# A hybrid decoder step on one core: an earlier count in the recurrent stage, and a first weight tile loaded by quarters

## The reference, cut to what matters

```python
def rmsnorm(x, g):
    y = xf * lax.rsqrt(jnp.mean(xf * xf, axis=-1, keepdims=True) + RMS_EPS)
    return (y * g).astype(x.dtype)
...
xn = rmsnorm(x, lp['g_mix'])
u = xn @ lp['w_in']
u_rw, u_ml, u_pool, u_gate = jnp.split(u, IN_SPLITS, axis=-1)
...
kk = k * k_k                                  # RWKV-7, per head of 64
kk = kk / jnp.maximum(jnp.sqrt(jnp.sum(kk * kk, axis=-1, keepdims=True)), 1e-12)
```

## Time and profile before

| | |
|---|---|
| median of 3 runs | 2074.45 us (2072.27 to 2074.98) |
| profiled execution | 2075.46 us, of which the span from first to last instruction 2073.7 us |
| mean granted TensorE clock | 0.956 |
| busy | PE 89%, weight loads 75%, DVE 46%, ACT 29%, POOL 19% of the span |
| front stage | 0 to about 479 us |
| recurrent stage | about 480 to 1160 us |

### The profile page before, as it was taken

How to read it: one execution, slowest core, us unless ns; L and a number is a source line. 1 busy time by engine, 2 the same in 40 slices (tenths; PEclk the granted TensorE clock), 3 DMA queues, 4 the chain that set the end, 5 groups by cost and what they waited for, 6 DMA issues and landing times. The chain is left out here.

```text
span 2073.7 us, 33699 instructions
## 1 busy us (share of the span) xinstructions
PE 1853.3 (89%) x13379; PEld 1549.4 (75%) x13379; DVE 944.5 (46%) x1521; ACT 596.7 (29%) x838; POOL 393.3 (19%) x362
## 2 busy tenths in 40 slices
PE   6999999998999999999999899999988877777775
PEld 6999999997777777877778799999977544443332
DVE  5553444546464563755646454545534122112113
ACT  3343223323133232332322433333434111000112
POOL 6550003112220212203212000084013000000002
PEclk9999999999999999999999999999998989888888
DMA  6445354434132222221221344543683999999995
GB/s 252 164 158 179 119 168 165 135 121 145 44 112 75 78 93 70 94 83 61 93 83 51 133 178 182 230 161 144 227 327 123 394 430 431 431 431 431 431 431 238
DMA packets 46168, 409.33 MB, mean 197 GB/s; under 512 B 6532, under 2 KB 8328, under 8 KB 16136
## 3 DMA queue, kind: packets, MB, share of 16 engines
q1 hardware_dynamic: 46088, 408.17, 50.9%
HBM read 396.98 MB, written 11.18 MB: 197 GB/s over the span
## 5 line engine op out<-in xcount | busy, mean ns | idle before, releaser
L375 PE MATMUL ps<-x_high,w_high 128*128 128x288 f32 x928 | 256.0, 302 | 16.2 <-ACT w_high L537 15.9
L376 PE MATMUL ps<-x_rest,w_high 128*128 128x288 f32 x928 | 252.0, 298 | 0.0
L375 PEld LDWEIGHTS ps<-x_high,w_high 128*128 128x128 f32 x928 | 176.4, 190 | 19.1 <-ACT w_high L537 16.4
L376 PEld LDWEIGHTS ps<-x_rest,w_high 128*128 128x128 f32 x928 | 176.3, 190 | 0.5
L537 ACT ACTIVATE w_high<-w_raw 128x2048 fp32r<-128x2048 f32 x58 | 111.0, 1915 | 164.8 <-DMA w_raw<-in_w_main 82.2
L643 DVE TENSOR_TENSOR w_rest<-w_raw,w_high 128x2048 fp32r<-128x2048 f32 x58 | 140.1, 2418 | 21.7 <-ACT w_high L537 21.5
L1105 PE MATMUL ps<-x_high,r_high 128*128 128x288 f32 x512 | 145.3, 309 | 0.0
L380 PE MATMUL ps<-x_high,w_rest 128*128 128x288 f32 x928 | 132.6, 295 | 2.2 <-DVE w_rest L643 2.2
L1590 POOL TENSOR_TENSOR xm<-ring,const 128x512 f32<-128x512 f32 x56 | 72.4, 1294 | 324.9 <-DVE ring L1487 232.2
L1105 PE MATMUL ps<-rx_low,r_high 128*128 128x288 f32 x480 | 130.8, 298 | 0.0
L380 PEld LDWEIGHTS ps<-x_high,w_rest 128*128 128x128 f32 x928 | 126.5, 189 | 2.4 <-DVE w_rest L643 2.4
(11 more groups left out here) (574 smaller groups left out, 4312.3 us busy)
## 6 DMA issues: line engine op xcount, KB each, us to landing
w_raw<-in_w_main SPq DMA_DIRECT2D x58, 1024.0 KB, 4.9
ring<-in_w_g SPq DMA_DIRECT2D x32, 1024.0 KB, 4.8
half_b<-in_w_egu SPq DMA_DIRECT2D x16, 2048.0 KB, 22.5
half_a<-in_w_egu SPq DMA_DIRECT2D x15, 2048.0 KB, 18.1
ring<-in_w_u SPq DMA_DIRECT2D x32, 512.0 KB, 3.5
ring<-in_w_gate SPq DMA_DIRECT2D x8, 2048.0 KB, 7.9
ring<-in_w_out SPq DMA_DIRECT2D x8, 2048.0 KB, 7.9
half_d<-in_w_egu SPq DMA_DIRECT2D x8, 2048.0 KB, 22.5
```

The lines of the kernel that those rows point to most:

```text
L375: mm(o, high[:, t % 2, k, :], x_h[:, k, :], start=(k == 0), stop=False)
L376: ins = mm(o, high[:, t % 2, k, :], x_l[:, k, :], start=False, stop=False)
```

## The change

In the front stage, x and the first weight tile are loaded in turns, a quarter of each; ACT rounds each quarter of the tile behind its quarter of x; and PE's first tile waits for quarters. The squares move from POOL (31 instructions) to one Square of 128x4608 on ACT, in place, behind the rounding of tile 2, and one reduction on DVE behind the rest of tile 2. In the recurrent stage DVE gives its first lap as its first instruction, and ACT's square of the key waits for `dxd` itself.

```diff
@@ stage_front
+        first_w, first_high = [sem(f"f_first{n}") for n in range(3)] + [slot[0]], sem("f_firsth")
@@ SP
             for n in range(4):
-                sp.dma_start(x[:, 4 * n:4 * n + 4, :], A["xT"][:, 4 * n:4 * n + 4, :]).then_inc(x_in[n], 16)
-            for t in range(SLOTS):
+                k = slice(4 * n, 4 * n + 4)
+                sp.dma_start(x[:, k, :], A["xT"][:, k, :]).then_inc(x_in[n], 16)
+                sp.dma_start(raw[:, 0, k, :].rearrange("p k n -> p (k n)"), A["w_main"][0, :, 512 * n:512 * n + 512]).then_inc(first_w[n], 16)
+            for t in range(1, SLOTS):
                 weights(t)
@@ PE
             def tile(t):
-                pe.wait_ge(w_high, t + 1)
+                if t:
+                    pe.wait_ge(w_high, t + 1)
...
                     if t == 0:
+                        pe.wait_ge(*((first_high, k // 4 + 1) if k < 12 else (w_high, 1)))
                         pe.wait_ge(x_high, k + 1)
                         pe.wait_ge(x_rest, k + 1)
...
-                    pe.wait_ge(squares, 2 * KD - 1)
+                    pe.wait_ge(squares, 2)
@@ ACT
-            for k in range(KD):
-                if k % 4 == 0:
-                    act.wait_ge(x_in[k // 4], 16)
-                fn(x_h[:, k, :], x[:, k, :], ACT.Copy, scale=par("g_mix", k)).then_inc(x_high, 1)
-            for t in range(-1, O0):
+            for n in range(4):
+                act.wait_ge(x_in[n], 16)
+                for k in range(4 * n, 4 * n + 4):
+                    fn(x_h[:, k, :], x[:, k, :], ACT.Copy, scale=par("g_mix", k)).then_inc(x_high, 1)
+                act.wait_ge(first_w[n], 16)
+                fn(high[:, 0, 4 * n:4 * n + 4, :], raw[:, 0, 4 * n:4 * n + 4, :], ACT.Copy).then_inc(w_high if n == 3 else first_high, 1)
+            for t in range(O0):
                 split(t + 1)
+                if t == 1:
+                    act.wait_ge(x_rest, KD)
+                    fn(x[:, :, :], x[:, :, :], ACT.Square).then_inc(squares, 1)
@@ DVE
             for t in range(SUM_AFTER + 2):
                 rest(t)
+                if t == 2:
+                    dve.wait_ge(squares, 1)
+                    nc.vector.tensor_reduce(rstd[:, :], x[:, :, :].rearrange("p k t -> p t k"), AX.X, ALU.add).then_inc(squares, 1)
@@ POOL
-            for k in range(KD):
-                if k % 4 == 0:
-                    pool.wait_ge(x_in[k // 4], 16)
-                if k == 0:
-                    tt(rstd[:, :], x[:, k, :], x[:, k, :], ALU.mult).then_inc(squares, 1)
-                    continue
-                pool.wait_ge(squares, 2 * k - 1)
-                tt(square[:, :], x[:, k, :], x[:, k, :], ALU.mult).then_inc(squares, 1)
-                pool.wait_ge(squares, 2 * k)
-                tt(rstd[:, :], rstd[:, :], square[:, :], ALU.add).then_inc(squares, 1)
@@ stage_rwkv, ACT, in the loop
                 split("00")
+                act.wait_ge(dxd, 6)
                 act.wait_ge(v.sem, v.at("o", i - 1))
                 a.done(fn(ekap, kk, ACT.Square), "kksq")
@@ stage_rwkv, DVE
+            dve.sem_inc(v.sem, v.n)
             ts(half[:, 0:KH], param[:, PARAM_AT["w0"]:PARAM_AT["w0"] + KH], 0.5, None, ALU.mult)
...
             dve.wait_ge(dxd, 6)
-            dve.sem_inc(v.sem, v.n)
             with dve.Fori(0, N) as i:
```

More of the change, by code:

```diff
@@ L231, in stage_front @@
         rstd = env["rstd"]
-        square, dn = placed("square", [P, T], "front", 10272), placed("dn", [P, T], "front", 10272)
+        dn = placed("dn", [P, T], "front", 10272)
         gt, nout = placed("gt", [P, 24], "front", 10560), placed("nout", [P, MLH, 9], "front", 10584)
```

## The result

The changed kernel takes 2062.18 us, the median of 4 runs (2058.43 to 2067.27); the kernel before, run beside it, 2073.88 (4 runs). The medians differ by 11.7 us, where 11.0 had been forecast (2063.4, range 2059.8 to 2067.9). The ratio is 0.9947 [0.9934, 0.9959], which is 11.0 us (8.5 to 13.7). The sum came out nearly right, but not its parts: both starts gained more than was said, and what was said to be handed on to the end was partly given back.

A forecast was written before the change was run, and what follows sets the result against it. PE was taken to bound the kernel, with only its idle time at the two edited places counting. Front 5.8 plus recurrent 5.2 gave 11.0 us off the 2074.45 median: 2063.4 us, range 2059.8 to 2067.9.

The forecast's parts named there:

- handed on to the end: Whole kernel: no transfer has a start of its own, so a shift of PE at the beginning reaches the end.
- The first tile by quarters: Front start: first quarter ready at 9.53 us, PE's low part of tile 0 at 19.0 against 24.84, 5.8 us earlier.
- I keep 10.1: Front, tile 0's low part to tile 2: 64 matmuls take 10.1 us as before; at full clock 8.5.
- the front's term: Gain of the whole front stage: 5.8 us, bounds 4.8 to 7.4.
- The reduction: Front, DVE before tile 3's rest: takes 9.6 us, covered by 3.1 us before PE wants that rest.
- The rival in which it is the new wait: Front: a slower reduction delays tile 3; at 7 ns an element the kernel is 8.5 us slower, 2083; chance 0.02.
- The recurrent term: Recurrent stage's start: `z` comes 5.2 us earlier, the middle of two measured clock patterns (4.6 and 5.8); bounds 1.8 to 6.5.
- ACT's chain, named as the cap: Recurrent stage's start: ACT's square of the key ends at 487.98 us, then tanh starts, capping the gain at 6.5 us.
- ACT's new wait: Recurrent stage, ACT's wait on `dxd`: already met when reached; a sequencer instruction costs 0.04 us, eight 0.3 us if unhidden.
- PE is held anyway: Recurrent stage's start: something the count covered up still holds PE; only the front's 5.8 us remain, 2068.6; chance 0.04.
- x's rest stays slow: Front, DVE: 958 ns is not POOL's doing, so the front gives only 0.5 us, 2068.7; chance 0.04.
- the clock stays low: Both starts stay at the lower clock: 0.5 us left in the front, 1.8 in the recurrent stage, 2072.1; chance 0.05.

The follow-up runs named there:

- front half alone: The changed kernel's front part only, with DVE's count for the recurrent stage where it was in the kernel before: 2067.70 us (12 runs), 0.9979 of the kernel before.
- the kernel with POOL's squares: The changed kernel with the squares given back to POOL and no reduction on DVE, quarters and early count kept: 2070.09 us (10 runs), 0.9982 of the kernel before.
- recurrent half: The changed kernel with all front edits undone, leaving DVE's early count and ACT's wait: 2066.95 us (9 runs), 0.9973 of the kernel before.
- the second profile of before: The kernel before, run and profiled again unedited: 2074.57 us (1 run).
- the third of the changed kernel: The changed kernel, unedited, profiled a third time: 2061.70 us (6 runs), 0.9952 of the kernel before.

## Why the prediction was right, and where it was not

*What bounds the kernel, and the mechanism of each half*: right. PE at the two edited places was what counted, x's rest was slow by POOL's squares, and DVE's count held PE.

*The first tile by quarters.* PE was forecast near 9.5 and began at 9.16 (x landed 0.4 us earlier); a quarter took 0.61 us (0.65), the low part began at 18.16 (19.0). Right, a little cautious.

*From there to tile 2.* "I keep 10.1" was the wrong choice of two bounds: it took 8.62, which is the other bound (8.5). The reason given, that the new low part too follows a stretch with gaps, did not hold. The pace rose at 14.7 us, in the third of the four quarters (12.5 and 14.9 us in the other two profiles), and the gaps of 0.4 and 1.0 us behind it did not bring it down. So the front's term of 5.8 (4.8 to 7.4) measured 8.2 at tile 2, outside its range: 0.8 from the start and 1.5 from the clock. At the stage's first load 8.1 are left in two profiles of the changed kernel, and 6.6 in the one whose clock fell near 197 us (6.5 in the front half alone). That pace and clock make the difference is borne out by the kernel with POOL's squares, where a wait of 1.89 us and slow matmuls stand again, and 8.1 us pass between the low parts of tiles 0 and 1 instead of 6.5.

*The reduction*: 8.74 against 9.6, and covered. The cover was 2.2 and not 3.1, since PE was earlier than forecast. The rival in which it is the new wait has the mechanism right: doubled, it costs 8.3 us.

*The recurrent term* of 5.2 (1.8 to 6.5) measured 5.5 to 5.9. The middle of two patterns of the clock was not the right way to size it. ACT's chain, named as the cap, is the bound at 8.8 us behind the stage's start, whether the clock is down there or not. ACT's new wait cost 0.05 us a lap at most: from the second on, laps without a fall take 84.39 to 84.48 us in the recurrent half and 84.35 to 84.42 in the kernel before. That is near the 0.04 that the prediction gave it, and too close to the spread to be told from nothing.

*The sum.* The step that failed is in the first paragraph: "a shift of PE at the beginning is handed on to the end". Of 14.0 us at r_rest, 13.4 and 8.8 are left at the stage's end, by the profiles of the changed kernel with one fall and with seven (1141.45 and 1146.06 against 1154.81, with two falls). No wait of PE over 0.4 us in the stage ended with a transfer. What took most of it is the granted clock in the laps, which differs from one execution to the next; but with one fall on either side (the second profile of before and the third of the changed kernel) 13.45 us at r_rest still become 11.85. That 11.0 agrees with 11.7 is luck in so far as the two errors have opposite signs. By the ratios of three sets the gain is 7.7, 9.9 and 11.0 us; the forecast lies above the interval of the first (5.2 to 10.4) and within the other two. Laps without a fall also take 84.5 us in the kernels that enter the stage before 476 us and 84.4 in those that enter it near 480, about 1 us over the stage. The front half alone, without ACT's new wait, has the 84.5 as well; the cause was not found.

*The rivals.* "PE is held anyway" and "x's rest stays slow" fell with the rows above; "the clock stays low" fell the other way round.

## What to carry to other kernels

Cut a first tile into pieces only when all else that the first matmuls wait for keeps up: here the quarters gave 0.3 us at most with x's rest slow and 3.9 with it fast. When a wait is removed, cost the chain that ends next, not the clock pattern of the engine that waited; here ACT's chain ended within 0.1 us of PE's. And before crediting a gain at the start to the end, count in more than one profile the stretches of lower clock in what follows: profiles of one code differed by up to 5 us at the end of this loop, as much as half of the change.

## What the runs showed of the hardware

- One code, entering a loop of eight laps at 471.45 and 471.46 us, had seven laps with a fall of the granted clock to 0.50 in one execution and one such lap in another. Each fall lasted 3.4 us, began behind the same stretch of small matmuls near the lap's end, and cost 0.8 us. Single runs of that code lay between 2056.95 us (mean granted clock 0.964) and 2068.19 us (0.951).
- A wait of 1.6 us in front of the norm at the lap's end, instead of 0.50, behind four larger matmuls instead of twelve, came with falls in every lap of two kernels.
- The same waits of 0.55 and 0.76 us in the front came with a fall of 3.4 us behind them in two profiles and with none in the others.
- The vector engine's instructions with two 128x288 inputs took 958 ns beside GpSimd's squares and 514 ns without them.
- In the first 14 us of the changed kernel's first profile the clock column read 1.00 while matmuls came every 0.24 us; the pace tells more there.
- 128x288 sums of 16 elements each, 1152 bytes apart, took 8.74 us, 1.90 ns per element read.
